# One block for the preparation of the gated delta rule, and a shorter first and last level of its triangular inverse

## The reference

```python
def pool_delta_mixer(h, w_in, pool_w, pool_scale, conv_w, a_log, dt_bias, o_norm, w_out):
    z = h @ w_in
    u, q, k, v, gate, beta_l, alpha_l = split_cols(z, A_SIZES)
    y_pool = multiscale_pool(u, pool_w, pool_scale)
    y_dn = gated_deltanet(q, k, v, gate, beta_l, alpha_l, conv_w, a_log, dt_bias, o_norm)
    return jnp.concatenate([y_pool, y_dn], axis=-1) @ w_out

# gated_deltanet: q, k are scaled to unit length (l2norm); then, per head and chunk of tokens
beta = sigmoid(beta_logit)
log_decay = -exp(a_log) * softplus(alpha_logit + dt_bias)
gc = cumsum(log_decay)
decay_mat = where(causal, exp(gc[:, None] - gc[None, :]), 0)
a_low = where(strict, (k * beta) @ k.T * decay_mat, 0)
t_mat = inverse(eye + a_low)                      # unit lower triangular
w_c = t_mat @ (k * beta * exp(gc)); u_c = t_mat @ (v * beta)
attn = where(causal, q @ k.T * decay_mat, 0)
# a scan over the chunks follows, then a norm, and the product with silu(gate)
```

## Time and profile before

| what | value |
|---|---|
| median of 3 runs | 3953.91 us (3953.71 to 3956.28) |
| the profiled execution's own time | 3953.35 us |
| its span, first to last instruction | 3951.5 us |
| mean granted TensorE clock | 0.950 |
| PE busy | 3618.6 us (92% of the span) |
| DVE busy | 1662.9 us (42%) |
| ACT busy | 1263.0 us (32%) |
| POOL busy | 181.1 us (5%) |

### The profile page before, as it was taken

The page is one execution under the profiler, slowest core; times in us unless marked ns, Lnnn a source line. Parts: engine busy times, 40 slices in busy tenths (PEclk is TensorE's granted clock), DMA queues, the critical chain, the costliest instruction groups (busy, mean ns, idle before and its releaser), DMA issues. The chain is left out here.

```text
span 3951.5 us, 45416 instructions
## 1 busy us (share of the span) xinstructions
PE 3618.6 (92%) x18186; PEld 2799.2 (71%) x18186; DVE 1662.9 (42%) x2713; ACT 1263.0 (32%) x2147; POOL 181.1 (5%) x282
## 2 busy tenths in 40 slices
PE   7879799999999999999987999799999888979999
PEld 5548587778755778777866745588887745757777
DVE  5343354433312655443335534344433435644443
ACT  3122243322212654332232111322222435642222
POOL 1023020100000002010000000000000001000000
PEclk9879899999999999999998999899999999989999
DMA  3326331222311003122230201111112300011222
GB/s 143 141 100 248 118 128 43 86 106 85 121 64 43 1 33 128 43 85 106 85 113 22 95 1 43 43 64 64 58 49 96 141 22 22 1 43 64 88 75 103
DMA packets 30057, 307.78 MB, mean 78 GB/s; under 512 B 3843, under 2 KB 5605, under 8 KB 9158
## 3 DMA queue, kind: packets, MB, share of 16 engines
q1 hardware_dynamic: 29894, 305.52, 20.8%
HBM read 303.41 MB, written 2.10 MB: 77 GB/s over the span
## 5 line engine op out<-in xcount | busy, mean ns | idle before, releaser
L562 PE MATMUL psum<-operand_rounded,weights_rest 128*128 128x512 f32 (+1 forms) x1360 | 521.7, 384 | 60.8 <-DVE operand_rest L533 60.8
L563 PE MATMUL psum<-operand_rounded,weights_rounded 128*128 128x512 f32 (+1 forms) x1360 | 519.0, 382 | 0.0
L564 PE MATMUL psum<-operand_rest,weights_rounded 128*128 128x512 f32 (+1 forms) x1360 | 518.0, 381 | 0.0
L531 DVE TENSOR_TENSOR weights_rest<-ring,weights_rounded 128x1024 fp32r<-128x1024 f32 x170 | 208.2, 1225 | 578.7 <-ACT operand_rounded L514 578.7
L327 PE MATMUL psum<-operand_rounded,weights_rest 128*128 128x512 f32 (+1 forms) x1056 | 380.3, 360 | 53.1 <-DVE weights_rest L346 53.1
L513 ACT ACTIVATE weights_rounded<-ring 128x1024 fp32r<-128x1024 f32 x170 | 179.9, 1058 | 633.8 <-PE psum L564 559.3
L328 PE MATMUL psum<-operand_rounded,weights_rounded 128*128 128x512 f32 (+1 forms) x1056 | 378.2, 358 | 0.0
L562 PEld LDWEIGHTS psum<-operand_rounded,weights_rest 128*128 128x128 f32 x1360 | 262.0, 193 | 113.3 <-issue 52.9
L564 PEld LDWEIGHTS psum<-operand_rest,weights_rounded 128*128 128x128 f32 x1360 | 261.9, 193 | 48.0
L563 PEld LDWEIGHTS psum<-operand_rounded,weights_rounded 128*128 128x128 f32 x1360 | 262.2, 193 | 47.1
L327 PEld LDWEIGHTS psum<-operand_rounded,weights_rest 128*128 128x128 f32 x1056 | 200.8, 190 | 89.9 <-issue 60.0
(11 more groups left out here) (440 smaller groups left out, 6412.6 us busy)
## 6 DMA issues: line engine op xcount, KB each, us to landing
ring<-in_ff_w SPq DMA_DIRECT2D x32, 2048.0 KB, 7.4
ring<-in_w_mod SPq DMA_DIRECT2D x24, 2048.0 KB, 7.5
ring<-in_ffn_up SPq DMA_DIRECT2D x22, 2048.0 KB, 7.4
ring<-in_ffn_down SPq DMA_DIRECT2D x33, 1024.0 KB, 4.8
ring<-in_a_w_in SPq DMA_DIRECT2D x4, 2048.0 KB, 11.2
ring<-in_xa_wk SPq DMA_DIRECT2D x4, 2048.0 KB, 7.3
ring<-in_xa_wv SPq DMA_DIRECT2D x4, 2048.0 KB, 8.2
ring<-in_xa_wq SPq DMA_DIRECT2D x4, 2048.0 KB, 7.4
```

The lines of the kernel that those rows point to most:

```text
L531: dve.tensor_tensor(parts["weights_rest"][:, r % 2, :], weight_rows(s, r), parts["weights_rounded"][:, r % 2, :].bitcast(F32), ALU.subtrac ...
L562: nc.tensor.matmul(k.bank(m, n), rest, top_in, start=first, stop=False)
L563: nc.tensor.matmul(k.bank(m, n), top, top_in, start=False, stop=False)
L564: mm = nc.tensor.matmul(k.bank(m, n), top, rest_in, start=False, stop=last)
```

## The change

The gate product and the blocks from delta_gates to the transposes of K and V become one block, `delta_prep`. Every engine has one written order through it, and semaphores per tile, head or group of four units take the place of the meetings. PSUM banks and arena regions are assigned anew so that the pieces can lie beside each other. It hosts 6 chunks of the modulations (before, 8), and the inverse hosts 14 in its even steps n = 0 to 26 (before, 12).

- The three exponentials over 2048 columns become exponentials over 512, one per group; the causal mask of attn is one 128x512 operation per group in place of four of 128x128.
- The mask of level 0 is made by POOL inside the new block, as soon as A is there. The multiplication of Q by its decay, on POOL, moves into levels 1 to 4 of the inverse. The 32 copies of the identity on POOL go.
- Level 0 of the inverse starts from the identity, so its products are replaced: X is the identity less the masked A, and its transpose the identity less a transpose of the masked A: 4 transposes and 2 DVE operations per group, no ACT copy. The last level updates only the transpose of X, so that 4 of its 8 second matmuls and one DVE operation per group go.

```diff
+def delta_prep(k, w, U, QKV, G, wba, pool_w, inv, small, regions, mods):
+    with nc.Block() as block:
+        @block.tensor
+        def _(pe):
+            # pe.wait_ge(*tables), then the 32 matmuls of 8 columns
+            pe.wait_ge(*gate_landed)
+            gate_tile(0)
+            for j in range(8):
+                pe.wait_ge(*squared.at(j + 1))
+                mm = nc.tensor.matmul(k.bank(1, SEQ, heads), strip[:, 15 - j:23 - j], squares[:, j, :], start=(j == 0), stop=(j == 7))
+            mm.then_inc(summed.sem, 1)
+            gate_tile(1)
+            pe.wait_ge(*v_step.at(12))
+            nc.tensor.matmul(running, k.c("upto"), ld, start=True, stop=True).then_inc(made.sem, 1)
+            gate_tile(2)
+            gate_tile(3)
+            mods.multiply(pe, 0)
+            pe.wait_ge(*refined.at(3))
+            pe.wait_ge(*v_step.at(13))
+            spread_of(0)
+            spread_of(1)
...
+            for c in range(4):
+                pe.wait_ge(*decayed.at(c + 1))
+                by_keys(kk_bank[c], K, c, kk)
+            mods.turn(pe, 2)
+            mods.multiply(pe, 3)
+            for c in range(4):
+                pe.wait_ge(*(pool_taken.at(c + 3) if c < 2 else a_made.at(c - 1)))
+                by_keys(qk_bank[c], Q, c, qk)
+            mods.turn(pe, 3)
+            mods.multiply(pe, 4)
+            for c in range(4):
+                pe.wait_ge(*(a_made.at(c + 3) if c < 2 else scaled.at(c - 1)))
+                turn(k_bank[c], K, c, k_turned)
+            mods.turn(pe, 4)
+            mods.multiply(pe, 5)
+            for c in range(4):
+                pe.wait_ge(*(scaled.at(c + 3) if c < 2 else k_taken.at(c - 1)))
+                turn(v_bank[c], V, c, v_turned)
+            mods.turn(pe, 5)
...
+        @block.vector
+        def _(dve):
...
+            for c in range(4):
+                dve.wait_ge(*qk.at(c + 1))
+                dve.wait_ge(*decaying.at(2 * c + 2))
+                nc.vector.tensor_tensor(four(attn, c), k.bank(qk_bank[c]), four(rise, c), ALU.mult).then_inc(scaled.sem, 1)
+                dve.wait_ge(*scaled.at(c + 1))
+                heads_of = four(attn, c).rearrange("p (h n) -> p h n", h=DN_HEADS)
+                nc.vector.tensor_tensor(heads_of, heads_of, repeat(k.c("upto")), ALU.mult)
+            mods.add(dve, 3)
+            for c in range(4):
+                dve.wait_ge(*k_turned.at(c + 1))
+                for h in range(4):
+                    j = c * 4 + h
+                    src = k.bank(k_bank[c])[:, h * P:(h + 1) * P]
+                    nc.vector.tensor_scalar(u128(kbg, j), src, ebg[:, j:j + 1], None, ALU.mult)
+                    op = nc.vector.tensor_scalar(u128(kdec, j), src, ekd[:, j:j + 1], None, ALU.mult)
+                op.then_inc(k_taken.sem, 1)
...
+        @block.gpsimd
+        def _(pool):
+            pool.wait_ge(*v_step.at(12))
+            for j in range(16):
+                op = nc.gpsimd.tensor_copy(u128(ldb, j), ld[:, j:j + 1].to_broadcast([P, P]))
+            op.then_inc(repeated.sem, 1)
+            pool.wait_ge(*tables)
+            for c in range(4):
+                pool.wait_ge(*a_made.at(c + 1))
+                for h in range(4):
+                    op = nc.gpsimd.tensor_tensor(u128(Aoff, c * 4 + h), u128(A, c * 4 + h), masks[:, 0:P], ALU.mult)
+                op.then_inc(masked.sem, 1)
...
-    hosted = {n: 8 + (n - 1) // 2 for n in range(1, 25, 2)}
+    hosted = {n: 6 + n // 2 for n in range(0, 28, 2)}
...
+                if level == 0:
+                    if n >= 2:
+                        pe.wait_ge(*updated.at(n - 1))
+                    for h in range(4):
+                        mm = nc.tensor.transpose(k.bank(b)[:, h * P:(h + 1) * P], u128(Aoff, c * 4 + h), k.c("ident"))
...
+                    if level < LEVELS - 1:
                         nc.tensor.matmul(k.bank(b + 1)[:, h * P:(h + 1) * P], u128(WTs, j), u128(Xi, j), start=True, stop=True)
...
+                if level == 0:
+                    dve.wait_ge(*masked.at(n + 1))
+                    nc.vector.tensor_tensor(by_unit(Xi, c), repeat(k.c("ident")), by_unit(Aoff, c), ALU.subtract)
+                    dve.wait_ge(*turned.at(n + 1))
+                    nc.vector.tensor_tensor(by_unit(XT, c), repeat(k.c("ident")), k.bank(b).rearrange("p (h n) -> p h n", h=DN_HEADS),
+                                            ALU.subtract).then_inc(updated.sem, 1)
```

More of the change, by code:

```diff
@@ L1344, in pool_delta_inputs @@
         counter.base += steps
-    def gate(act, chunk, m, g, bank, before):
-        act.activation(G[:, g, :], bank[:, 0:512], ACT.Silu).then_inc(drained.sem, 1)
-    product(k, "a_w_gate", lambda t, s, n: k.h[:, t, s:s + n], [(i * P, P) for i in range(TT)], scalar=gate,
-            stationary="tokens")
-def delta_gates(k, wba, beta, ld, gcol, tmp, mods):
+def delta_prep(k, w, U, QKV, G, wba, pool_w, inv, small, regions, mods):
     nc = k.nc
-    made, a_step, v_step = k.counter("gates_product"), k.counter("gates_act"), k.counter("gates_dve")
+    Q, K, V = QKV[:, 0:4, :], QKV[:, 4:8, :], QKV[:, 8:12, :]
+    A, attn, kdec, kbg, vb, dec, erow, rise, Aoff, masks = regions
+    beta, ld, gcol, tmp = small[:, 0:16], small[:, 16:32], small[:, 32:48], small[:, 48:144]
+    egc, ekd, ebg = (small[:, 192 + i * 16:208 + i * 16] for i in range(3))
@@ new lines, in delta_prep @@
+    work = [k.region(18688 + i * 512, 512) for i in range(2)]
+    mean, squares, rows = k.region(19712, 4, 512), k.region(22784, 8, 512), k.region(14592, 4, 512)
+    ldb = attn
+    strip, heads = k.c("strip"), slice(0, 8)
+    made, a_step, v_step = k.counter("gates_product"), k.counter("delta_act"), k.counter("delta_dve")
+    gated, silu = k.counter("product_ready"), k.counter("bank_drained")
+    p_step, meaned, pooled, pool_taken = k.counter("conv_step"), k.counter("pool_mean"), k.counter("pool_product"), k.counter("values_used")
@@ L1387, in _ @@
             mods.condition(act)
+            nc.scalar.preload_act_table_set(LN_AND_EXP)
+            for j in range(8):
+                nc.scalar.activation(squares[:, j, :], QKV[:, j, :], ACT.Square).then_inc(squared.sem, 1)
             step = Chain(act, a_step)
@@ L1398, in _ @@
+            decays(2)
+            decays(3)
+            nc.scalar.activation(ekd, ekd, ACT.Exp).then_inc(tail.sem, 1)
+            for c in range(3, 6):
+                mods.copy(act, c)
+            for c in range(4):
+                act.wait_ge(*v_turned.at(c + 1))
+                for h in range(4):
+                    j = c * 4 + h
+                    op = nc.scalar.activation(u128(vb, j), k.bank(v_bank[c])[:, h * P:(h + 1) * P], ACT.Copy, scale=beta[:, j:j + 1])
         @block.vector
@@ L1412, in _ @@
                                                     in1=ea[:, 0:4], op0=ALU.mult, op1=ALU.mult))
-            mods.add(dve, 0)
-            mods.add(dve, 1)
-            dve.wait_ge(*made.at(2))
-            step(nc.vector.tensor_copy(gcol, k.bank(1, 16)))
+            window(2)
+            dve.wait_ge(*root.at(3))
+            r = [rows[heads, i, :] for i in range(4)]
+            refine(nc.vector.tensor_scalar(r[2], k.bank(1, SEQ, heads), 1.0, EPS, ALU.mult, ALU.add))
+            refine(nc.vector.scalar_tensor_tensor(out=r[3], in0=r[0], scalar=-0.5, in1=r[2], op0=ALU.mult, op1=ALU.mult))
@@ new lines, in _ @@
+            refine(nc.vector.scalar_tensor_tensor(out=r[2], in0=r[3], scalar=1.5, in1=r[1], op0=ALU.add, op1=ALU.mult))
+            dve.wait_ge(*made.at(2))
+            step(nc.vector.tensor_copy(gcol, running))
+            window(3)
+            for j in range(8):
+                dve.wait_ge(*spread.at(j + 1))
+                nc.vector.scalar_tensor_tensor(out=QKV[:, j, :], in0=k.bank(j % 4), scalar=float(P) ** -0.5 if j < 4 else 1.0,
+                                               in1=QKV[:, j, :], op0=ALU.mult, op1=ALU.mult).then_inc(normed.sem, 1)
```

523 lines of the change are left out of this document (208 added, 315 removed).

## The result

| what | before | after |
|---|---|---|
| median | 3953.81 us (4 runs, 3953.2 to 3956.28) | 3891.01 us (4 runs, 3888.19 to 3893.15) |
| the profiled execution, its span | 3953.35, 3951.5 us | 3888.19, 3886.4 us |
| mean granted clock | 0.950 | 0.956 |

The kernel before ran once more beside it, so its median is 0.1 under that of the table ahead of the change. The ratio is 0.984, its 95% interval 0.9823 to 0.9857: 1.6% faster. Forecast were 3888 us and a range of 3873 to 3908.

What follows compares the result with a forecast made beforehand. Preparation was taken as bound by edges and low clock, the inverse by PE's work. Gains of 54.0 and 12.2 made 66.2 us, from 3953.91 to 3887.7, said as 3888; range 3873 to 3908.

Steps and rivals of the forecast that it cites:

- The idle time and the path: Preparation: bound by edges and low clock; merged into one block it takes 103.7 us in place of 157.7.
- 8 columns 12.5, gate tile 10.0: Start of the block: 8-column products keep their old price, 12.5 us; first gate tile 10.0 as before; 22.5 together.
- Sums of squares 6.9; two to four gate tiles, running sum and multiply 22.8: Block, behind the first gate tile: PE's work from there to the end of the first multiply, reaching 52.2 us.
- Spreads 14.0: Block, behind the first multiply: 8 copies of a row to all partitions stay at the low clock, 14.0 us, reaching 66.2.
- To the first Q K group 85.9: Block: PE's summed path from its start through decays, pool products and K K products to first Q K group, 85.9 us.
- attn 7.1, K 8.4: End of the block on DVE: four groups of attn 7.1 us with POOL contention, 32 scalings of K 8.4.
- DVE last: End of the block: DVE is late, not PE; PE's transposes and ACT's scaling of V end a little sooner.
- The inverse 109.0: Inverse: 109.0 us in place of 121.2, a gain of 12.2, nearly all from level 0 and the last level.
- fall in the second half of the block: First rival: from the pool products on, short groups with waits run at the low clock; +15 us, 3903; chance 15%.
- stay down: Fourth rival: the clock stays at 1.2 GHz through block and inverse; about +98 us, 4052; chance 3%.
- The plain rule of activity: Second rival: the spreads run at 2.4 GHz since nothing idles ahead of them; -6.5 us, 3881; chance 12%.
- The chain of small waits: Third rival: PE waits for DVE and ACT inside the merged block, which needs 120 to 130 us; +20, 3908; chance 9%.

Runs made afterwards that it cites:

- three edges: The kernel after with three all-engine edges put back into the new block (before the spreads, the K K products, the transposes of K): 3894.91 us, ratio 0.9846.
- full rows: The kernel after with the eight spreads over all 128 rows (120 of them zero) in place of 8 rows: 3881.07 us, ratio 0.9813.
- gate first: The kernel after with gate tile 0 ahead of the 32 products of 8 columns, these in one piece: 3888.60 us, ratio 0.9834.
- gate in edge: The kernel after with gate tile 0 moved ahead of the edge that opens the new block: 3884.40 us, ratio 0.9816.
- wide scalings: The kernel after with scalings of K and V as 128x512 operations, leaving out three of four heads' factors: 3887.32 us, ratio 0.9825.
- block only: The kernel after with the old inverse, all seven levels full: 3897.93 us, ratio 0.9857.

## Why the prediction was right

The forecast 3888 was 3.0 us under the median of 3891.01, and for the profiled execution it was 1.0 under (3953.35 - 66.2 = 3887.2 against 3888.19). Point by point, from the start of the block (123.86):

- **The idle time and the path.** Right: no wait of PE is listed between the edges, and the block took 102.9 us for 103.7. But the cause was half understood. I wrote that the preparation is bound by edges; the run with three edges shows that the meetings there cost 5 us of idle time, 7 in the layer, where the waits had been 17.1, and 11.3 us of the old waits lay inside blocks. What is left as the cost before is that each block held little beside one chain; that part is an inference from what the edges do not cost.
- **8 columns 12.5, gate tile 10.0.** 13.6 and 9.9. I took the old price, whose window read 0.55; here all is at 0.50.
- **Sums of squares 6.9; two to four gate tiles, running sum and multiply 22.8.** 7.0 and 22.9.
- **Spreads 14.0.** Half right. Alone they took 10.8: four at 2.4 GHz, four at 1.2 GHz. The turn among them and the two groups of decays behind them paid instead, so that up to the end of these decays I had 68.9 and it was 69.6. That rows in use, not waits, decide is shown by the run with full rows. The Trainium skill (TensorE: Matmul & The Clock Gate, What's actually happening) lets activity release the throttle; the spreads and the 8-column products kept PE busy 100% and fell from 1.00 to 0.50, so busy time in a profile is not that activity. That was my reading of one row, and the runs "full rows", "gate first" and "gate in edge" now bear it out.
- **To the first Q K group 85.9.** 87.6 (211.42 - 123.86). The 1.5 for hand-overs, which I added at the end, is spent here; from DVE's last addition to the inverse passed 0.8, where I had 0.5.
- **attn 7.1, K 8.4.** 6.0 and 8.4. Only one of four masks ran beside POOL and took 1.37; POOL was done before the others. I had charged all four.
- **DVE last.** Right but for ACT, which I had ending sooner: it ended 0.1 us later. The run with wide scalings moved the end by 1.8 us and no more, since PE is that close behind.
- **The inverse 109.0.** 107.2. The low start, 1.5, was not there in this profile (it was in others, 0.74 in "block only"); the weights' wait, 2.0, was 0.8; level 0 took 8.2 for 8.0; the last pairs 6.57 for 6.6. I also had POOL idle while level 0 subtracts the masked A; it was at its masks from 228.18 on, and two of the four subtractions took 0.92 and 0.76 us for 0.69, which cost nothing that the waits list. Both halves were also priced alone: 12.7 for the inverse, 57.1 for the block.
- **Behind the layer.** Here the sum had no term. 69.1 us at the end of the inverse became 67.5 within 3 us, and 65.1 at the end of the span. My 66.2 for the change was 2.9 too small, and the loss behind made up for it. Of the 2.9, some 1.0 is the preparation (55.0 for 54.0) and the rest the inverse. This is chance, not insight.
- **The rivals.** The clock did not fall in the second half of the block (28.1 us at 1.00), nor stay down. The plain rule of activity came true in the first four spreads alone. The chain of small waits left no listed wait.

What stays open: what the old order would cost without its edges; why the same edge leaves the inverse at 1.00 in one kernel and lower in another, where PE idles 2.8 us in both; and what in the later stages decides where the low level begins. Both move single results by 2 to 4 us, as the kernel before does by itself from run to run (3950.46 to 3956.94 in nine executions).

## What to carry to other kernels

Merge stages to put independent work beside a chain, more than to save the meetings, three of which cost 7 us here: count what PE has to do while the others work. Then look at the granted clock of every stretch in which PE is "busy": matmuls of few rows or few moving columns run for long in one piece were paid twice here, once themselves and once in the dense work behind them. What helped here was to fill the rows up with zeros, to cut the piece up between dense tiles, and to fill an edge with a tile that is ready.

## What the runs showed of the hardware that was not expected

- 8 matmuls of 8x512, four ahead of a turn and four behind it, with no gap listed on PE: the clock fell from 0.99 to 0.50 between the fours. The same with 128 rows: 1.00 throughout, and 3.7 us for each four, where the low level took 7.2.
- Matmuls with 8 columns of weights and 128 rows (the sums of squares, 6.9 us in one piece) stayed at 1.00. So few output partitions did no harm; few input rows or few moving columns did.
- The fall comes late and is paid late: in the kernel after, a turn (1.87 us for 0.95) and two groups of decays stand in the low stretch that the spreads caused.
- A piece of 8-column products, 1.8 us long, did not bring the clock down between dense tiles, but behind an edge it was followed by 4 us at 0.64 for the first part of the next gate tile.
